# Modulation and decode projection from unsplit 32-bit weights, in four column strips

## What is computed

```python
mod = einsum('bd,de->be', silu(c), w['w_ada']) + w['b_ada']   # 9 rows (8 decode, 1 prompt), 1024 -> 6144
sh1, sc1, ga1, sh2, sc2, ga2 = split(mod, 6)
h = rms(x, norm1_g) * (1.0 + sc1) + sh1                       # 1024 prompt rows, 8 decode rows
z = h @ w['w_in']                                             # of it here: 8 decode rows x 1944 columns
```

## Time and profile before

| | us |
|---|---|
| median of 3 runs | 2084.87 |
| lowest, highest run | 2082.83, 2086.28 |
| span of the profiled execution | 2086.2 |
| last instruction of `modulation_and_h` ends (DVE, L364) | 143.46 |
| first gate matmul of `gates_and_decode` | 149.19 |

### The profile page before, as it was taken

The page is one execution under the profiler, slowest core; times in us unless marked ns, Lnnn a source line. Parts: engine busy times, 40 slices in busy tenths (PEclk is TensorE's granted clock), DMA queues, the critical chain, the costliest instruction groups (busy, mean ns, idle before and its releaser), DMA issues. The chain is left out here.

```text
span 2086.2 us, 34791 instructions
## 1 busy us (share of the span) xinstructions
PE 1972.7 (95%) x13032; PEld 1856.5 (89%) x13032; DVE 1163.0 (56%) x2531; ACT 678.2 (33%) x1273; POOL 152.2 (7%) x190
## 2 busy tenths in 40 slices
PE   5889999999997799999998999999999999999997
PEld 4658798789996688898898999999999999999997
DVE  4944333334244677777775546655556565555555
ACT  5623243331223566666573133311111110101011
POOL 1442100101300100000200000000000000000000
PEclk8799999999998899999899999999999999999999
DMA  9776453521001000000003541221212020211102
GB/s 311 255 215 205 152 180 98 156 94 60 30 26 66 1 1 1 1 1 1 1 1 102 173 131 50 62 61 30 60 30 60 30 60 30 60 31 59 40 0 82
DMA packets 151758, 157.10 MB, mean 75 GB/s; under 512 B 15859, under 2 KB 132483, under 8 KB 151604
## 3 DMA queue, kind: packets, MB, share of 16 engines
q1 hardware_dynamic: 140076, 130.73, 20.4%
q0 software_dynamic: 4656, 16.40, 2.3%
q10 hardware_dynamic: 6912, 8.46, 1.1%
HBM read 139.33 MB, written 18.32 MB: 76 GB/s over the span
## 5 line engine op out<-in xcount | busy, mean ns | idle before, releaser
L1877 DVE SCALAR_TENSOR_TENSOR l_x2T<-tail_bank,g_modT,l_x2T 128x344 f32<-128x344 f32 (+1 forms) x528 | 265.3, 566 | 101.5 <-PE tail_bank L1614 101.3
L1614 PE MATMUL tail_bank<-l_wo 128*128 128x344 f32 x1584 | 270.2, 319 | 1.8 <-DVE late_total_s L1883 1.8
L1614 PEld LDWEIGHTS tail_bank<-l_wo 128*128 128x128 f32 x1584 | 252.7, 188 | 2.0 <-issue 2.0
L1448 ACT ACTIVATE l_act<-tail_bank 128x344 f32<-128x344 f32 x66 | 30.2, 457 | 523.6 <-PE tail_bank L1596 523.6
L884 PE MATMUL nsa_out<-zs_z,nsa_probT 128*128 128x64 f32 (+1 forms) x1344 | 176.1, 277 | 5.3 <-DVE zs_z L1040 5.1
L884 PEld LDWEIGHTS nsa_out<-zs_z,nsa_probT 128*128 128x128 f32 x1344 | 169.1, 198 | 7.1 <-DVE zs_z L1040 7.0
L1596 PE MATMUL tail_bank<-late_words_hi,l_uhi 128*128 128x344 f32 x528 | 169.7, 321 | 3.3 <-DVE late_words_lo L1780 3.3
L1596 PE MATMUL tail_bank<-late_words_lo,l_uhi 128*128 128x344 f32 x528 | 169.3, 321 | 0.0
L1596 PE MATMUL tail_bank<-late_words_hi,l_ulo 128*128 128x344 f32 x528 | 169.2, 320 | 0.0
L1596 PE MATMUL tail_bank<-late_words_lo,late_wo 128*128 128x344 f32 x528 | 169.1, 320 | 0.0
L1596 PE MATMUL tail_bank<-late_words_hi,l_wo 128*128 128x344 f32 x528 | 169.1, 320 | 0.0
(11 more groups left out here) (504 smaller groups left out, 4329.2 us busy)
## 6 DMA issues: line engine op xcount, KB each, us to landing
mod_wr<-in_w_ada SPq DMA_DIRECT2D x24, 1024.0 KB, 5.3
kin_kin<-in_cache_kv SPq DMA_DIRECT2D x64, 256.0 KB, 3.4
late_gate<-in_w_ffn_in SPq DMA_DIRECT2D x22, 512.0 KB, 5.7
l_raw_o<-in_w_ffn_out SPq DMA_DIRECT2D x22, 512.0 KB, 3.6
late_raw<-in_w_ffn_in SPq DMA_DIRECT2D x22, 512.0 KB, 5.4
gate_d<-dec_gate ACTq DMA_DIRECT2D x48, 172.0 KB, 2.9
late_gate<-gate_d SPq DMA_DIRECT2D x8, 1032.0 KB, 5.5
dec_vin<-in_cache_kv SPq DMA_DIRECT2D x64, 128.0 KB, 2.2
```

The costliest lines, as they stand in the source:

```text
L1448: act.activation(sg[(j + c) % 2], pg[(j + c) % 2][:, 0:TCH], ACT.Silu).then_inc(silu_done, 1)
L1614: mm = pe.matmul(po[u % 4][:, 0:TCH], w[j][:, k * P:(k + 1) * P], a[j][:, tok(c)], start=(q == 0), stop=(q == 2))
L1877: mm = dve.scalar_tensor_tensor(out=here, in0=po[u % 4][:, 0:part_w(c)], scalar=g.modT[:, 5 * KD + k, NDEC:NC9], in1=here, op0=ALU.mult, o ...
```

## The change

The stage no longer splits the `w_ada` pieces. `c` stays in 32 bits, in 32 columns of which 9 are used and the others are zero (`c32`); `hs` is widened to 32 columns in the same way. The eight 128-row blocks of a piece go in turn to four strips of 32 PSUM rows (`grouped`), two blocks per strip, so that a piece leaves four partial sums of 9 (or 8) rows. `pick` becomes 128 x 9 with ones at rows r, 32+r, 64+r and 96+r, and the turning product adds the four strips. For the decode rows, which were not turned, a product with `pick` is added (`z_rows`) before the copy to `g.zd`. Pieces are 512 columns (12 of `w_ada`, 2.1 MB each) and 486 columns (4 of `w_in`), in four buffers that come free when their matmuls are done (`mod_ps`). ACT's roundings and DVE's differences of the pieces are gone; ACT squares the tiles of `x` as they land. `x` is loaded once the first piece has landed. The row scales and all eight row products are made at piece 5, and the 16 units run four to a piece from piece 6 to 9.

```diff
-    WC = 256
+    WC = 512
-    ZC = ZW // 8
+    NQ = WC // P
+    ZC = ZW // 4
-    RAWS, SPLITS = 3, 3
-    RATE, UNIT0 = 8, 11
+    RAWS = 4
+    GROUPS, GW = 4, 32
+    AT_SCALE, AT_ROWS, AT_UNITS, PER_STEP = 4, 5, 6, 4
...
-        c18 = s.sb("c18", [P, KD, 2 * NC9], F32R)
-        pick = s.sb("pick", [2 * NC9, NC9])
-        mod = [s.sb(f"mod{i}", [2 * NC9, WC]) for i in range(2)]
+        c32 = s.sb("c32", [P, KD, GW])
+        pick = s.sb("pick", [P, NC9])
+        mod = [s.sb(f"mod{i}", [P, WC]) for i in range(2)]
...
+        units_at = lambda m: range(max(0, m - AT_UNITS) * PER_STEP, min(2 * KD, (m - AT_UNITS + 1) * PER_STEP)) if m >= AT_UNITS else range(0)
...
             def _(sp):
                     if m >= RAWS:
-                        old = m - RAWS
-                        if old < NMOD:
-                            sp.wait_ge(w_lo, old + 1)
-                        else:
-                            sp.wait_ge(z_ps, old - NMOD + 1)
+                        sp.wait_ge(mod_ps, m - RAWS + 1)
...
             def _(pool):
-                pool.wait_ge(w_in[1], 16)
+                pool.wait_ge(w_in[0], 16)
...
             def _(act):
-                for m in range(NMOD):
-                    loaded(act, m)
-                    if m >= SPLITS:
-                        act.wait_ge(mod_ps, m - SPLITS + 1)
-                    act.activation(whi[m % SPLITS][:], wr[m % RAWS][:], ACT.Copy).then_inc(w_hi, 1)
...
             def _(pe):
+                def grouped(out, rows, m, n):
+                    pe.wait_ge(w_in[m % RAWS], m // RAWS * 16 + 16)
+                    for k in range(KD):
+                        j = k % GROUPS
+                        mm = pe.matmul(out[j * GW:(j + 1) * GW, 0:n], rows[:, k, :], wr[m % RAWS][:, k, 0:n],
+                                       start=(k < GROUPS), stop=(k >= KD - GROUPS))
+                    return mm
...
-                    for q in range(2):
+                    for q in range(NQ):
                         mm = pe.matmul(pq[:, q, :], mod[m % 2][:, q * P:(q + 1) * P], pick[:], start=True, stop=True)
...
+                def z_rows(i):
+                    pe.wait_ge(z_sb, i + 1)
+                    ...
+                    pe.matmul(pick_ps[0:NDEC, 0:ZC], pick[:, 0:NDEC], mod[i % 2][:, 0:ZC], start=True, stop=True).then_inc(zrow_ps, 1)
...
                 for m in range(NMOD):
-                    pe.wait_ge(w_lo, m + 1)
                     if m >= 3:
                         pe.wait_ge(mod_sb, m - 2)
-                    for k in range(KD):
-                        for q, b in enumerate((whi, wlo)):
-                            mm = pe.matmul(pm[m % 3][:], c18[:, k, :], b[m % SPLITS][:, k, :], start=(k == 0 and q == 0), stop=(k == KD - 1 and q == 1))
-                    mm.then_inc(mod_ps, 1)
+                    grouped(pm[m % 3], c32, m, WC).then_inc(mod_ps, 1)
                     if m:
                         mod_transposed(m - 1)
-                    if m == UNIT0:
+                    if m == AT_UNITS:
                         pe.wait_ge(xn_done, 1)
                         ...
-                    turned(unit_at(m))
+                    for u in units_at(m):
+                        turned(u)
...
-                    for k in range(KD):
-                        mm = pe.matmul(pm[m % 3][0:NDEC, 0:ZC], hs[:, k, :], wr[m % RAWS][:, k, 0:ZC], start=(k == 0), stop=(k == KD - 1))
-                    mm.then_inc(z_ps, 1)
-                    turned(unit_at(m))
+                    grouped(pm[m % 3], hs, m, ZC).then_inc(z_ps, 1)
+                    if i:
+                        z_rows(i - 1)
+                z_rows(NZ - 1)
...
             def _(dve):
                 for m in range(NMOD):
-                    dve.wait_ge(w_hi, m + 1)
-                    dve.tensor_tensor(wlo[m % SPLITS][:], wr[m % RAWS][:], f32(whi[m % SPLITS][:]), ALU.subtract).then_inc(w_lo, 1)
...
                 for i in range(NZ):
                     dve.wait_ge(z_ps, i + 1)
                     ...
-                    dve.tensor_copy(g.zd[:, i * ZC:(i + 1) * ZC], pm[(NMOD + i) % 3][0:NDEC, 0:ZC]).then_inc(z_sb, 1)
-                    high_h(unit_at(NMOD + i, 3))
+                    dve.tensor_copy(mod[i % 2][:, 0:ZC], pm[(NMOD + i) % 3][:, 0:ZC]).then_inc(z_sb, 1)
+                    if i:
+                        z_row(i - 1)
+                z_row(NZ - 1)
```

More of the change, by code:

```diff
@@ L123, in modulation_and_h @@
         aT = s.sb("aT", [P, KD, NC9])
-        hs = s.sb("hs", [P, KD, NDEC])
+        hs = s.sb("hs", [P, KD, GW])
+        hd = hs[:, :, 0:NDEC]
         pc = s.ps("pc", [P, KD, NC9])
-        pm = [s.ps(f"pm{i}", [2 * NC9, WC]) for i in range(3)]
+        pm = [s.ps(f"pm{i}", [P, WC]) for i in range(3)]
         pt = [s.ps(f"pt{i}", [P, 512]) for i in range(3)]
-        pq = s.ps("pq", [P, 2, NC9])
+        pick_ps = s.ps("pick_ps", [P, 512])
+        pq = pick_ps[:, 0:NQ * NC9].rearrange("p (q r) -> p q r", q=NQ)
         c_in, rows_in, w_in = s.sem("c_in"), s.sem("rows_in"), [s.sem(f"w_in{i}") for i in range(RAWS)]
@@ L178, in _ @@
                 pool.dma_start(xs, io["x_sample"].rearrange("b t d -> (b t) d")).then_inc(xs_in, 16)
-                def low_h(u):
+                for u in range(2 * KD):
                     half, k = half_of(u), k_of(u)
@@ L184, in low_h @@
                     pool.tensor_tensor(g.hT_lo[:, k, cols], hf[:, u % 3, :], f32(g.hT_hi[:, k, cols]), ALU.subtract).then_inc(h_lo, 1)
-                for u in range(2 * KD):
-                    low_h(u)
             @block.scalar
             def _(act):
-                def square(t):
+                act.wait_ge(c_in, 32)
+                act.activation(c9[:], c9[:], ACT.Silu).then_inc(silu_done, 1)
+                act.wait_ge(zeroed, 1)
+                for t in range(TT + 1):
+                    if t:
+                        act.wait_ge(sq_done, t)
                     if t == TT:
@@ L198, in square @@
                         act.activation(junk, x[:, t, :], ACT.Square, accum_out=ssq[:, t:t + 1]).then_inc(sq_done, 1)
[L200 to L212, removed]
-                for m in range(NMOD):
-                    loaded(act, m)
-                    if m >= SPLITS:
-                        act.wait_ge(mod_ps, m - SPLITS + 1)
-                    act.activation(whi[m % SPLITS][:], wr[m % RAWS][:], ACT.Copy).then_inc(w_hi, 1)
[L218 to L227, removed]
+                act.wait_ge(rstd_done, 1)
+                act.activation(rstd[:], rstd[:], ACT.Sqrt).then_inc(std_done, 1)
+                act.wait_ge(coef, 1)
+                for u in range(2 * KD):
+                    k = k_of(u)
+                    act.wait_ge(h_ps, u + 1)
+                    if u >= 3:
+                        act.wait_ge(h_lo, u - 2)
+                    act.activation(hf[:, u % 3, :], pt[u % 3][:], ACT.Identity, bias=g.modT[:, k, NDEC:NC9],
+                                   scale=aT[:, k, NDEC:NC9]).then_inc(h_sb, 1)
             @block.tensor
@@ L280, in _ @@
                     m = NMOD + i
-                    loaded(pe, m)
                     if i < 3:
@@ L312, in mod_biased @@
                     dve.wait_ge(modT_ps, m + 1)
[L313 to L314 removed]
+                    cols = slice(NQ * m, NQ * (m + 1))
+                    dve.tensor_tensor(g.modT[:, cols, :], pq, biasT[:, cols].unsqueeze(2).broadcast_to([P, NQ, NC9]), ALU.add).then_inc(modT_sb, 1)
                 def normalised(t):
@@ L319, in high_h @@
                 def high_h(u):
-                    if u is not None:
-                        half, k = half_of(u), k_of(u)
-                        dve.wait_ge(h_sb, u + 1)
-                        dve.tensor_copy(g.hT_hi[:, k, half * 512:half * 512 + 512], hf[:, u % 3, :]).then_inc(h_hi, 1)
+                    half, k = half_of(u), k_of(u)
+                    dve.wait_ge(h_sb, u + 1)
+                    dve.tensor_copy(g.hT_hi[:, k, half * 512:half * 512 + 512], hf[:, u % 3, :]).then_inc(h_hi, 1)
                 def decode_h():
```

81 lines of the change are left out of this document (42 added, 39 removed).

## The result

The changed kernel took 2054.41, 2055.39, 2060.09 and 4222.94 us in four executions (median 2057.74); the last, more than twice as long for no reason that the record shows, is a slow one and is left out of what follows, which leaves a median of 2055.39. The kernel before took 2085.57 us beside it (median; 2082.83 to 2091.39). The ratio is 0.9849, 95% interval 0.9826 to 0.9871: 1.5% faster. The profiled execution has a span of 2053.6 us, 32.6 us shorter than before. The forecast was 2065 us with a range of 2047 to 2084. The time lies in it, but it lies at the place of the first rival, four strips abreast, which had been worked out at 2052 us of time, or 2053.5 of span.

What follows compares the result with a forecast made beforehand. DVE and PE set the first stage's pace in turn while DMA waits; afterwards PE is late. Stage end 143.5 to 124.3 is -19.2, with the hand-over -19.9: span 2066.3, less 1.3, 2065 us; range 2047 to 2084.

Steps and rivals of the forecast that it cites:

- the first rival: First stage: strips don't wait for each other's second pass, the DMA queue bounds, end 111.5 us, 2052 us; chance 0.26.
- The group: PE's 16 passes per weight piece: taken as 9 slots, 3.93 us, between 1.75 and 6.98 us.
- The lower bound: PE's passes for one piece with four strips abreast: 4 slots, 1.75 us.
- the pairs: Main case: a strip's second pass runs beside the next strip's first, 3.93 us a group, 2065 us; chance 0.42.
- The sum for the pairs: PE's chain from piece 6: 57.6 + 66.7 = 124.3 us stage end, including 2 us for stalls.
- From span to time: Whole kernel: 1.3 us taken off the forecast span, as the profile's span lay above the median of three runs.
- The weight loads: PE in the stage: the skill's rule makes same-row loads come one after another; the trace shows loads inside running matmuls.
- The rival's 111.5 us: Stage end with four strips abreast: last piece at 107.5, plus 1.7 last group, 1.3 copies, 1.0 `z_rows`.
- Units, turning and buffers: Stage terms: POOL 1.28 to 1.7 us per unit, turning 1.1 us, four buffers keeping 17 us of transfer in hand.
- The slow clock: Rival: PE idles between groups and the clock halves, a pairs group takes 7.86 us, 2081 us; chance 0.12.
- The hand-over: Behind the stage: the 3.7 us `graw0` wait goes, the next wait takes most; 0.7 us gain, between 0 and 3.7.
- The third rival: First stage: strips don't run at once, 6.98 us a group, PE bounds, end 162 us, 2103 us; chance 0.17.

Runs made afterwards that it cites:

- strip by strip: Changed kernel with four strips, but the program lists all four passes of one strip one after the other: 2059.51 us.
- Two strips: Changed kernel with a piece's blocks alternating between two strips of PSUM rows instead of four: 2060.78 us.
- one strip: Changed kernel with all eight blocks of a piece in a single strip of 32 PSUM rows instead of four: 2103.92 us.
- three buffers: Changed kernel with three weight buffers in place of four: 2054.61 us.
- the second execution: The changed kernel itself, unedited, timed and profiled again beside variants on the same chip: 2057.91 us, ratio 0.9857.
- small pieces: Changed kernel with pieces of 256 (243) columns in eight buffers, so packets of 1 KB instead of 2 KB: 2071.72 us.

## Why the prediction was right, and where it was wrong

**What bounds, and the sign: right.** DVE's splits and PE's decode products held the queue back; with both gone it runs without a pause up to 98 us.

**The group: wrong.** The step that failed reads "if PE starts its instructions in order, the second pass of a strip has to wait for the first, and only the second pass of one strip runs beside the first of the next. That is 9 slots, 3.93 us. I take this one". I took it because one matmul's two passes stand strictly one behind the other. That row shows one strip, and it says nothing on whether the next strip's matmul waits for the second pass. It does not: 4 slots, 1.92 us, and strip by strip shows that even four listed passes hold nothing up. The lower bound, 1.75 us, was the nearer one, and with it the first rival came true. The time fell into the stated range because that range took in the rival; the range given for the pairs alone, 2060 to 2076, misses the 2055.39.

**The sum for the pairs: too long as well.** Two strips tests its other terms. PE's chain from the first group of the unit steps (56.71 us) to the stage's end (113.42) takes 56.7 us there, where the prediction's terms make 62.4 for eight slots. A turning took about 1.0 us for 1.3, four units 2.2 for 2.6, and the 2 us of stalls did not come. An estimate from this run for nine slots adds 4.3 us for ten groups: a stage end near 118, not 124.3, and a span near 2060. So even with groups of 3.93 us the forecast would have been some 6 us too high, and the total time alone, with its scatter of several us, hardly tells pairs from four abreast. The length of the group does.

**From span to time: the wrong way.** The prediction took 1.3 us off the span. In every later run the time is 1.8 us above the span of the same execution (2055.39 and 2053.6). By this the profiled execution of the kernel before, with its span of 2086.2 us, was slower than the three that were timed, and part of the 32.6 us between the spans is this: the medians of the times lie 30.2 us apart.

**The weight loads: the trace's side held.** The row in which loads lay inside running matmuls of the same strip spoke against loads that wait, and one strip shows it for whole groups: 16 passes in 7.05 us leave no room for 16 loads of 0.11 us each (PEld's mean there is 114 ns). The Trainium skill ("TensorE: Matmul & The Clock Gate", Part 3: Packing small matmuls — row/col tiling) also says that matmuls start and end strictly in the order given; by the count of slots above that would be near 5.7 us a group for strip by strip, and the run, at 1.94 us, disagrees.

**The rival's 111.5 us came out at 111.22, by two errors that cancel.** The rate was 387 GB/s, not 370. By that the last piece should land at 12.3 + 35.2/0.387 = 103.3 us; it landed at 104.44, since the 8.0 MB of `w_in` come in packets of 1944 bytes, at 365 to 367 GB/s from 83 to 98 us. Behind it I put 1.7 + 1.3 + 1.0 = 4.0 us. It took 6.6: the group ran at the lower clock (3.36), and the product of the last `z` row waited 0.84 us for the copy of the row ahead, which reads the same bank.

**Units, turning and buffers: right, or free.** POOL took 1.39 us a unit (1.28 to 1.7 taken), a turning 1.06 (1.1). The eight row products of DVE took 5.37 us from 56.13, inside the slack of the queue. Four buffers were to cover PE's lateness; three buffers shows that at 1.92 us a group three are enough. Whether 3.93 us would need the fourth was not tried.

**The slow clock: seen, and harmless there.** It was 0.50 from 60 to 65 us, in the first unit step, which the prediction named as a sign against itself. That sign was wrong: with pieces in hand and more transfers queued (DMA share 1.05), a group of 3.64 us costs nothing. It cost 1.5 us in one place, the last group of one execution.

**The hand-over: right, with one sign off.** Forecast 0.7 us, measured 32.91 - 32.24 = 0.67 (0.3 in the second execution). DVE's wait for `graw0` went from 3.72 us to 0.32 of waiting for the stage's end; in the second execution it waits 1.37 us for `graw0`. So this load has "landed before DVE asks" in one of the two only; it lies at the tail of a full queue. The wait for the queries grew from 3.51 to 6.55 us, as put, since DVE's path runs through POOL's load behind the stage (114.55, 3.3 us behind its end). But it is not the first wait of PE there, as I had it: ahead of it lie 3.0 us for DVE's split of `graw0` (6.2 in the waits of before). The one fell by 3.2, the other grew by 3.0.

**The third rival: right in its mechanism, near in its price.** The group came as worked out, 7.05 us for 6.98. The stage ended at 158.36 us where 162 had been worked out, so that the total meets (2103 and 2103.9 us) partly by chance.

## What to carry to other kernels

Where matmuls have few rows of output, try to spread them over column strips. Here that divided their time nearly by the number of strips (3.63 us for two, 1.92 for four, in place of 7.05), for 32-bit products of two passes too. Work that only served to make the matmuls cheap may then be dropped. Work out the time for the case that everything on the engines is hidden, that is, bytes over the rate of a queue that never pauses; if an engine's group fits behind that, its exact length no longer matters, nor does its clock. Count the size of the packets among the changes: larger pieces were worth 7 to 8 of the 32 us. After such a gain look at the first waits behind the stage: the one for the queries lay on the path, and a wait of PE of 6 us cost its length and some slow work behind it.

## What the runs showed of the hardware that was not expected

Four 32-bit matmuls of 128 x 32 weights in different column strips run at the same time, 1.92 us against 7.05 for 16 passes of 512 columns (3.67 times), whether the program lists the strips in turn or one strip's four passes first. The rate of a full DMA queue was 349 GB/s with packets of 1 KB and 387 with 2 KB, and already 367 with packets of 1944 bytes. A wait of PE of 4.4 to 6.6 us was followed by 5 us of work at the 1.2 GHz level in eight executions of eight; filling most of the wait gave back 1.2 to 2.4 us of it.

One number misleads. In strip by strip the groups before 56 us took 3.67 us, the length at the lower level, while PEclk says 1.00 from 30 to 56 us. The clock record of that trace begins at 54.0 us (15.5 us in the changed kernel's), and a stretch without a record is shown as 1.00, so that this 1.00 is no measurement. The record of small pieces begins at 72.3 us: its half-size groups took 1.93 us before and 1.07 from then on.
